# The last expert's result, the final norm and the output rows, done by column halves

## The reference

```python
def _rmsnorm(x, g):
    y = xf * lax.rsqrt(jnp.mean(xf * xf, axis=-1, keepdims=True) + NORM_EPS)
    return (y * g).astype(x.dtype)

def _moe(h, w_router, w_gate, w_up, w_down):
    ...
    for e in range(N_EXPERTS):
        y = y + gates[:, e:e + 1] * _swiglu(t, w_gate[e], w_up[e], w_down[e])

x = x + _moe(...)               # layer 1
return _rmsnorm(x, g_final)     # (1, 256, 1024)
```

## Time and profile before

| engine | busy us | share of the span |
|---|---|---|
| PE | 1409.1 | 97% |
| DVE | 1203.9 | 83% |
| ACT | 1014.6 | 70% |
| POOL | 79.8 | 6% |

### The profile page before, as it was taken

How to read it: one execution, slowest core, us unless ns; L and a number is a source line. 1 busy time by engine, 2 the same in 40 slices (tenths; PEclk the granted TensorE clock), 3 DMA queues, 4 the chain that set the end, 5 groups by cost and what they waited for, 6 DMA issues and landing times.

```text
span 1446.1 us, 18577 instructions
## 1 busy us (share of the span) xinstructions
PE 1409.1 (97%) x7175; PEld 1187.1 (82%) x7175; DVE 1203.9 (83%) x1298; ACT 1014.6 (70%) x1239; POOL 79.8 (6%) x87
## 2 busy tenths in 40 slices
PE   7999999999999999999999999999999999999997
PEld 5788999997788788888888888888888888888885
DVE  5886555556976889999999999998999999999996
ACT  4664544444664678878888888887888888888884
POOL 1210000000210210000010010000000000000000
PEclk9999999999999999999999999999999999999999
DMA  8532951353433999999999999999999999999970
GB/s 294 203 117 95 381 181 59 117 183 117 175 117 125 400 392 396 381 395 391 377 373 390 379 371 388 381 363 394 384 373 380 387 377 373 387 383 364 394 272 31
DMA packets 187403, 435.24 MB, mean 301 GB/s; under 512 B 7886, under 2 KB 14772, under 8 KB 187316
## 3 DMA queue, kind: packets, MB, share of 16 engines
q1 hardware_dynamic: 183748, 421.93, 78.6%
q0 software_dynamic: 3136, 10.54, 2.5%
q10 hardware_dynamic: 432, 1.57, 0.3%
HBM read 426.66 MB, written 7.37 MB: 300 GB/s over the span
## 4 chain that ended last, share of the span: by engine, by line
PE 90%; DVE 4%; DMA 3%; SPq 1%; ACT 1%; issue 0%; POOL 0%; POOLq 0%; ACTq 0%
PE ps L1705 82%; DMA slot_rows<-facts,slot_i 2%; PE ps L2055 2%; PE ps L1795 1%; PE ps L1830 1%; DVE split L1438 1%; DMA ring_a<-in_w_in 1%; DVE E L1249 1%; DVE E L1267 1%; PE ps L1811 1%; DMA hn<-hn_rows,meta 1%; DVE neg_max L1252 1%; PE ps L2028 0%; SPq L675 0%; PE ps L1896 0%
## 5 line engine op out<-in xcount | busy, mean ns | idle before, releaser
L1705 PE MATMUL ps<-split,hTs 128*128 128x512 f32 (+2 forms) x3456 | 801.7, 390 | 6.6 <-DVE split L1438 3.8
L1705 PEld LDWEIGHTS ps<-split,hTs 128*128 128x128 f32 x3456 | 638.4, 189 | 135.4 <-DVE split L1438 6.3
L1438 DVE TENSOR_TENSOR split<-ring_a,split 128x1024 fp32r<-128x1024 f32 (+2 forms) x480 | 573.5, 1213 | 100.1 <-ACT split L1013 38.3
L1024 ACT ACTIVATE split<-ring_a 128x1024 fp32r<-128x1024 f32 x384 | 406.0, 1061 | 96.2 <-PE ps L1705 96.0
L1438 DVE TENSOR_TENSOR split<-ring_b,split 128x1024 fp32r<-128x1024 f32 x322 | 388.3, 1223 | 73.3 <-ACT split L1013 37.7
L1705 PE MATMUL ps<-split,acts 128*128 128x512 f32 x1608 | 379.6, 392 | 1.5 <-DVE acts L1438 1.5
L1024 ACT ACTIVATE split<-ring_b 128x1024 fp32r<-128x1024 f32 x288 | 304.3, 1063 | 76.1 <-PE ps L1705 75.1
L1705 PEld LDWEIGHTS ps<-split,acts 128*128 128x128 f32 x1608 | 301.0, 188 | 66.8 <-DVE acts L1438 1.9
L1705 PE MATMUL ps<-hTs,split 128*128 128x256 f32 x1056 | 128.2, 283 | 0.8 <-DVE hTs L1438 0.8
L1705 PEld LDWEIGHTS ps<-hTs,split 128*128 128x128 f32 x1056 | 127.5, 190 | 1.6 <-DVE hTs L1438 1.3
L896 ACT ACTIVATE split<-ring_a 128x1024 fp32r<-128x1024 f32 (+2 forms) x64 | 60.1, 976 | 20.2 <-DMA ring_a<-in_w_in 13.9
(11 more groups left out here) (190 smaller groups left out, 592.2 us busy)
## 6 DMA issues: line engine op xcount, KB each, us to landing
ring_a<-in_w_exp_gate SPq DMA_DIRECT2D x32, 2048.0 KB, 10.9
ring_a<-in_w_exp_up SPq DMA_DIRECT2D x32, 2048.0 KB, 11.6
ring_a<-in_w_exp_down SPq DMA_DIRECT2D x32, 2048.0 KB, 11.1
ring_b<-in_w_exp_gate SPq DMA_DIRECT2D x24, 2048.0 KB, 9.7
ring_b<-in_w_exp_up SPq DMA_DIRECT2D x24, 2048.0 KB, 11.1
ring_b<-in_w_exp_down SPq DMA_DIRECT2D x24, 2048.0 KB, 10.7
ring_a<-in_w_in SPq DMA_DIRECT2D x8, 2048.0 KB, 9.0
ring_a<-in_w_out SPq DMA_DIRECT2D x4, 2048.0 KB, 11.4
```

The costliest lines, as they stand in the source:

```text
L1024: act.activation(ex_unit(v)[0], ex_part(c, u), ACT.Copy).then_inc(hi_done, 1)
L1438: dve.tensor_tensor(dst, src, high.bitcast(F32), ALU.subtract).then_inc(signal, 1)
L1705: ins = pe.matmul(dst, a[ia], b[ib], start=(first and i == 0), stop=(last and i == 2))
```

## The change

- **PE, last chunk** (`last_item_down`): for the last expert's last down chunk the loops are turned round. All four units are multiplied into half 0 first (12 matmuls, counted by `last_ps`), then into half 1 (12 matmuls, which count `unit_done`).
- **ACT** (`last_item_out`) scales half 0 when `last_ps` is counted. DVE scales half 1 as before.
- **PE, `add_last`**: half 0 of both tiles, then half 1 of both tiles. Half 0 waits for ACT's result alone.
- **DVE, `add_last`**: the four additions to x in that order; half 0 counts `half_back`.
- **ACT, `last_squares`**: four instructions of 512 columns, each with a sum of its own; the 1/1024 of the mean is in the scale of the square.
- **POOL** multiplies half 0 of both tiles by the gains, before the factor is known (`half_gain`). DVE does so for half 1 of tile 1.
- **DVE** adds the two sums and epsilon with one small instruction a tile (`mean_sum`); POOL takes the power -0.5 of that, with no instruction ahead of it.
- **The rows**: ACT multiplies half 0 of tiles 0 and 1 by the factor (`out_a`). DVE waits for both factors and then does half 1 of tile 1 (by the factor), and half 1 of tile 0 (by the factor and the gains in one) (`out_d`).
- **SP, `first_store`**: four stores of 256 KB (128 rows of 2 KB), in the order tile 0 half 0, tile 1 half 1, tile 1 half 0, tile 0 half 1, each behind its own count.
- A new small tile `mean_h` stands after `rstd`, so that the tiles declared after it lie a little higher. The semaphore counts for the second round are adapted.

```diff
+        mean_h = sb("mean_h", [P, TILES])
...
+            def first_store():
+                rows = out[0].rearrange("(t p) d -> p t d", p=P)
+                for done, n, t, h in ((out_a, 1, 0, 0), (out_d, 1, 1, 1), (out_a, 2, 1, 0), (out_d, 2, 0, 1)):
+                    sp.wait_ge(done, n)
+                    sp.dma_start(rows[:, t, xcols(h)], hn[:, t, xcols(h)]).then_inc(stored, 16)
...
             reload()
-            norm(2 * DEPTH)
+            pool.wait_ge(grow_in, 32)
+            for t in range(TILES):
+                pool.wait_ge(half_back, t + 1)
+                pool.wait_ge(back_ps, 2)
+                pool.tensor_tensor(hn[:, t, xcols(0)], x[:, t, xcols(0)], g_row[:, xcols(0)], ALU.mult).then_inc(half_gain, 1)
+            for t in range(TILES):
+                pool.wait_ge(mean_sum, t + 1)
+                pool.tensor_tensor(rstd[:, 2 * DEPTH, t:t + 1], mean_h[:, t:t + 1], half_neg[:, 0:1], ALU.pow).then_inc(rstd_done, 1)
...
+            def last_item_out():
+                act.wait_ge(last_ps, 1)
+                act.wait_ge(scattered, 16 * scatters_before(LAST_ITEM))
+                act.activation(ex_out[:, xcols(0)], ps[:, 2, :], ACT.Copy, scale=gate_of(LAST_ITEM)).then_inc(last_out, 1)
+            def last_squares():
+                junk = hT[:, :, :].rearrange("p c n -> p (c n)")
+                for h in range(2):
+                    for t in range(TILES):
+                        if h:
+                            act.wait_ge(x_done, 2 * (2 * DEPTH - 1) + t + 1)
+                        else:
+                            act.wait_ge(half_back, t + 1)
+                        a = (2 * h + t) * FW
+                        act.activation(junk[:, a:a + FW], x[:, t, xcols(h)], ACT.Square, scale=D_MODEL ** -0.5,
+                                       accum_out=sumsq[:, 2 * DEPTH, t:t + 1] if h else mean_h[:, t:t + 1],
+                                       ).then_inc(sq_done if h else half_sq, 1)
+            def last_rows():          # ACT
+                for t in range(TILES):
+                    act.wait_ge(half_gain, t + 1)
+                    act.wait_ge(rstd_done, TILES * 2 * DEPTH + t + 1)
+                    act.activation(hn[:, t, xcols(0)], hn[:, t, xcols(0)], ACT.Copy,
+                                   scale=rstd[:, 2 * DEPTH, t:t + 1]).then_inc(out_a, 1)
...
             def add_last():           # DVE, after the product with the gate
+                for h in range(2):
+                    for t in range(TILES):
+                        dve.wait_ge(x_back[t], 16)
+                        dve.wait_ge(back_ps, 2 * h + t + 1)
+                        dve.tensor_tensor(x[:, t, xcols(h)], x[:, t, xcols(h)], ps[:, 4 * t + h, :],
+                                          ALU.add).then_inc(x_done if h else half_back, 1)
+            def last_rows():          # DVE
+                dve.tensor_tensor(hn[:, 1, xcols(1)], x[:, 1, xcols(1)], g_row[:, xcols(1)], ALU.mult).then_inc(last_gain, 1)
+                for t in range(TILES):
+                    dve.wait_ge(half_sq, t + 1)
+                    dve.wait_ge(sq_done, TILES * n + t + 1)
+                    dve.scalar_tensor_tensor(mean_h[:, t:t + 1], mean_h[:, t:t + 1], EPS, sumsq[:, n, t:t + 1],
+                                             ALU.add, ALU.add).then_inc(mean_sum, 1)
+                dve.wait_ge(rstd_done, TILES * (n + 1))
+                dve.tensor_scalar(hn[:, 1, xcols(1)], hn[:, 1, xcols(1)], rstd[:, n, 1:2], None, ALU.mult).then_inc(out_d, 1)
+                dve.scalar_tensor_tensor(hn[:, 0, xcols(1)], x[:, 0, xcols(1)], rstd[:, n, 0:1], g_row[:, xcols(1)],
+                                         ALU.mult, ALU.mult).then_inc(out_d, 1)
...
+            def last_item_down():     # PE
+                pe.wait_ge(actl_done, n + 1)
+                for h in range(2):
+                    for q in range(4):
+                        if h == 0:
+                            units.append(unit(LAST_ITEM, EX_POS[("d", j)], q))
+                        ins = three(ps[:, 2 + h, :], [ex_actTs[n % 2][:, p, q, :] for p in range(2)],
+                                    [p[:, xcols(h)] for p in units[q]], False, q == 3)
+                        if h:
+                            ins.then_inc(unit_done, 1)
+                    if h == 0:
+                        ins.then_inc(last_ps, 1)
...
             def add_last():           # PE
-                pe.wait_ge(eo_done, 2 * EXPERTS)
-                for t in range(TILES):
-                    for h in range(2):
+                for h in range(2):
+                    if h:
+                        pe.wait_ge(eo_done, 2 * EXPERTS)
+                    else:
+                        pe.wait_ge(last_out, 1)
+                    for t in range(TILES):
                         pe.matmul(ps[:, 4 * t + h, :], sel[:, t, :], ex_out[:, xcols(h)],
                                   start=True, stop=True).then_inc(back_ps, 1)
```

More of the change, by code:

```diff
@@ L539, in build @@
         eo_done = sem("eo_done")
+        last_ps, last_out = sem("last_ps"), sem("last_out")
+        half_back, half_sq, half_gain = sem("half_back"), sem("half_sq"), sem("half_gain")
+        last_gain, mean_sum, out_a, out_d = sem("last_gain"), sem("mean_sum"), sem("out_a"), sem("out_d")
         scattered = sem("scattered")
@@ L707, in expert_items @@
                     expert_chunk(last, EXPERTS - 1, c)
+            def first_store():
[3 more added lines that the diff above has]
+                    sp.dma_start(rows[:, t, xcols(h)], hn[:, t, xcols(h)]).then_inc(stored, 16)
             def store(r):
                 for t in range(TILES):
-                    sp.wait_ge(out_ready, r * TILES + t + 1)
+                    sp.wait_ge(out_ready, (r - 1) * TILES + t + 1)
                     sp.dma_start(out[0].rearrange("(t p) d -> p t d", p=P)[:, t, :], hn[:, t, :]).then_inc(stored, 16)
@@ L717, in _ @@
             count = sp.value_load(most_i[0:1, 0:1], min_val=0, max_val=SEQ)
-            store(0)
-            sp.wait_ge(stored, 16 * TILES)
+            first_store()
+            sp.wait_ge(stored, FIRST_STORED)
             for r in range(1, ROUNDS):
@@ L724, in _ @@
                     store(r)
-                    sp.wait_ge(stored, 16 * TILES * (r + 1))
+                    sp.wait_ge(stored, FIRST_STORED + 16 * TILES * r)
         @block.gpsimd
@@ L825, in second_round @@
                 pool.wait_ge(xy_again, 16 * TILES)
-                pool.wait_ge(stored, 16 * TILES)
+                pool.wait_ge(stored, FIRST_STORED)
                 first = r * EXPERTS
@@ L1087, in put_out @@
                     if i == LAST_ITEM + 1:
-                        act.wait_ge(stored, 16 * TILES)
+                        act.wait_ge(stored, FIRST_STORED)
                     elif scatters_before(i):
@@ L1116, in expert_items @@
                         expert_chunk(i, EX_CHUNKS)
-                    put_out(i, 0)
+                    if i == LAST_ITEM:
+                        last_item_out()
+                    else:
+                        put_out(i, 0)
                 if last != LAST_ITEM:
                     put_out(last, 1)
+            def last_item_out():
[20 more added lines that the diff above has]
+                                   scale=rstd[:, 2 * DEPTH, t:t + 1]).then_inc(out_a, 1)
             def final_squares(n):
                 for t in range(TILES):
[L1123 to L1127, removed]
+                    act.wait_ge(x_back[t], 16 * (n - 2 * DEPTH + 1))
+                    act.wait_ge(scattered, 16 * scatters_before(ITEMS))
                     squares(n, t)
@@ L1137, in _ @@
             expert_items(0)
-            final_squares(2 * DEPTH)
+            last_squares()
+            last_rows()
             act.wait_ge(count_done, 1)
@@ L1617, in add_last @@
                 dve.wait_ge(scattered, 16 * LAST_ITEM)
-                dve.tensor_scalar(ex_out[:, xcols(1)], ps[:, 3, :], gate_of(LAST_ITEM), None, ALU.mult).then_inc(eo_done, 1)
-                for t in range(TILES):
-                    dve.wait_ge(x_back[t], 16)
-                    for h in range(2):
-                        dve.wait_ge(back_ps, 2 * t + h + 1)
-                        ins = dve.tensor_tensor(x[:, t, xcols(h)], x[:, t, xcols(h)], ps[:, 4 * t + h, :], ALU.add)
-                    ins.then_inc(x_done, 1)
+                dve.tensor_scalar(ex_out[:, xcols(1)], ps[:, 3, :], gate_of(LAST_ITEM), None, ALU.mult).then_inc(eo_done, 2)
+                for h in range(2):
[5 more added lines that the diff above has]
+            def last_rows():
+                n = 2 * DEPTH
+                dve.wait_ge(grow_in, 32)
+                dve.wait_ge(x_done, 2 * n)
+                dve.tensor_tensor(hn[:, 1, xcols(1)], x[:, 1, xcols(1)], g_row[:, xcols(1)], ALU.mult).then_inc(last_gain, 1)
+                for t in range(TILES):
+                    dve.wait_ge(half_sq, t + 1)
[3 more added lines that the diff above has]
```

(17 more changed lines are left out.)

## The result

The changed kernel takes 1453.59 us (median of 6 executions, 1452.75 to 1456.29); the kernel before, on the same chip, 1449.33 (6 executions, 1445.55 to 1452.79). The ratio is 1.0037 with a 95% interval of 1.0023 to 1.0051: slower by more than the 0.2% that can be told apart. The forecast of 1448.8, with a range up to 1451.0, was wrong.

What follows compares the result with a forecast made beforehand. PE, busy 97%, was taken to bound the kernel, so only the tail behind the last down product could move. The steps there summed to -0.73, rounded to -0.7: median 1449.5 to 1448.8 us, range 1446.7 to 1451.0.

Steps and rivals of the forecast that it cites:

- part 8: Stores: four pieces of 0.65 us back to back, data ending at 1442.91 against 1443.64, gain 0.73; moved tiles counted as nothing.
- Rival D: Something away from the tail, the moved tiles or added code, costs or gives more than 2.9 us; chance 6%.
- if the time before the last chunk differs: Sign that the forecast is wrong: any difference in the time ahead of the last chunk, where nothing was to be won.
- part 1: PE's last chunk, first half first: a new stall of 0.62 us; last product starts at 1432.55 against 1431.93.
- Part 2: The sel products on PE need no wait for half 0: start at 1432.78 instead of 1433.26, gain 0.48 us.
- Part 3: Squares of 512 columns beside DVE's additions: the fourth ends at 1437.93 against 1438.85, 0.92 us gained in all.
- Part 4: POOL's gain products ahead of the factor: 1.17 us each (bounds 1.16 to 2.36), ending at 1435.97 and 1437.15.
- Rival C: POOL's gain products take 2.36 us each, so POOL is late and the kernel slower, 1451.1; chance 10%.
- Parts 5 and 6: DVE's gain product costs nothing, small additions end at 1438.27; POOL's two powers of 0.55 us end by 1439.33, against 1440.14.
- Part 7: Final rows: ACT's two end at 1440.13, DVE's last at 1440.63 against 1441.45, 0.82 us gained.
- Rival A: The last small store closes like the first store, so the end lands 1.1 us sooner: -1.8, 1447.7; chance 20%.
- rival B: Nothing is left: store pieces need 0.85 us each, or a stall of 1.1 eats the sel gain; 1449.5; chance 17%.

Runs made afterwards that it cites:

- unit by unit: Changed kernel with mean_h behind all tiles, 64 unused bytes between ring_b and acts, and the last chunk in its old order: 1442.69 us, ratio 0.9976 to the kernel before.
- both changes: Changed kernel with mean_h behind all other tiles and 64 unused bytes between ring_b and acts: 1442.99 us, ratio 0.9972 to the kernel before.

## Why the prediction was wrong

**The step that failed** is the last sentence of part 8: "The tile `mean_h` moves later tiles by a few bytes; no row speaks for a cost, and I count nothing." The runs put 6.8 us in its place (1608 products, 4.2 ns each), of which 0.7 comes back at the gate and up products; with the tile or a gap alone the medians rose by 5.1 to 5.7. With it fell the first paragraph's "nothing is to be won before the last chunk". Rival D named the moved tiles, and had 6% for lack of a row. The sign "if the time before the last chunk differs" came true, and the one on gaps in the stores' data did too. That no row showed a cost was no evidence that there was none: no kernel with the tile elsewhere had been traced, so the cost was unknown on both sides, and the range should have said so. One row could have raised the question. Two kinds of product with one shape, the gate/up and the down products, were 1.5 ns apart (227.5 and 229.0), and part 1 took the 0.229 as what a product costs.

**The tail**, which the prediction worked out, gained 0.47 where 0.73 was forecast. Step by step, after less 6.6 against the forecast:

- Part 1: PE goes on behind the low part at 1429.27, forecast 1429.34. The stall was there, and smaller: the ninth and the tenth product start 0.61 apart, so it is 0.38 beyond the usual interval, forecast 0.62. The run unit by unit shows that it was not needed: counting half 0 early is enough.
- Part 2: the `sel` products start at 1432.87, forecast 1432.78; the fourth addition ends at 1437.26, forecast 1437.18.
- Part 3: the squares end at 1438.01, forecast 1437.93.
- Part 4: POOL's two products take 1.25 each, forecast 1.17, and end at 1444.02, 0.06 behind the start of DVE's own product. Rival C's 2.36 did not come, which fits a wait for DVE in its bare row, as the neighbours in the earlier trace rows said.
- Parts 5 and 6: the small additions end at 1438.27, as forecast, and the powers at 1439.30, forecast 1439.33.
- Part 7: ACT's rows end at 1440.19, forecast 1440.13; DVE's last at 1440.48, forecast 1440.63.
- Part 8: here most of the 0.26 was lost. What did not hold is "an issue takes 0.36, so SP keeps up". Data began at about 1447.07, which is 1440.47 on the forecast's axis, against 1440.31: 0.16 late. They did not follow each other without a gap: the stretch from 1447.40 on has a DMA share of 0.82, where full ones have 1.01 to 1.03. The third and the fourth issue came late: the four stood 16.15, 16.55, 17.48 and 17.95 behind the transposes, and with the tile elsewhere 16.09, 16.49, 16.97 and 17.46. The second issue itself took 0.88 here and 0.43 there (issue ns, min/median/max, after and with the tile elsewhere):

```profile
L718 SPq DMA_DIRECT2D out<-hn x4: 360/643/884, 1446.2 to 1448.0; - x4
```
```profile
L718 SPq DMA_DIRECT2D out<-hn x4: 360/442/455, 1442.4 to 1443.7; - x4
```

  With both changes it took 1.03, unit by unit 0.43. Why it varies, no run shows. The end of the bulk of the data, near 1450.1, is 1443.5 on that axis: 0.6 behind the forecast of 1442.91. The landing was quicker than I assumed, and gave part of that back: the four stores landed 2.4 to 3.4 behind their issue, against 3.8 for the second store in the earlier trace rows. (The prediction's 1440.95 for the last issue does not follow from a row that is ready at 1440.63; the sum does not use it. The last issue stood at 1441.42.)

Rival A is not borne out in the sum (0.47, not 1.8), nor rival B (part 7's gain came, and the order by halves did not eat it).

The tail of 21.84 in the run with the tile elsewhere is 0.78 shorter than before, close to the 0.73 of the forecast. Ten traces have the tail of before, with 22.41 to 22.78; the three with the edited one have 21.84 to 22.15. The median there, 1448.2 against 1448.04, shows no gain; 0.05% is under what a measurement can tell. So the tail's gain is read from traces, and no time shows it.

## What to carry to other kernels

A declared tile is an edit to every tile behind it: before an added buffer is costed at nothing, look which operands of the hot loop it shifts against each other, and put small tiles behind the large ones. When a time changes, first compare the distance from start to start of the commonest instruction in both traces; here that and the busy time of the group gave the place of the loss at once, while the busy shares (97% both times) and the waits were silent. A gap of a few unused bytes is a cheap experiment, and here it won more (3.75 us in the median) than the whole rewritten tail (0.47 to 0.78, in traces alone).

## What the runs showed of the hardware

Products of 128 x 128 by 512 in this kernel start every 226.9 ns when the weights' tile and the streamed tile start at the same offset modulo 256 bytes, every 229.0 with the weights 64 bytes lower, and every 232.9 to 233.4 at the four other distances tried. Moving both together changes nothing, and the intervals stay apart where no other engine and no transfer is at work. The weight load's own duration doesn't show it (a mean of 187 ns for `acts` and 188 for `hTs` after). The Trainium skill (TensorE: Matmul & The Clock Gate, section "Step-by-step: what each phase is for") says that PE has two independent SBUF read ports, so that loading the next weights takes no read bandwidth from the running matmul. By that alone the place of the two tiles would not matter; here it matters by up to 6.5 ns in 227, and the measurement decides. Why it is 256 bytes, and whether the load and the stream meet in the memory or elsewhere, no run here shows.
